# A two-layer kernel on one core: the context rows' expert products at 256 columns a strip instead of 128

## The chip, the cores and the metric

The kernel runs on one core of a Trainium2 chip. TensorE multiplies, VectorE, ScalarE and GpSimd do the rest, SyncE starts most of the transfers. The metric is the device time of one execution in microseconds (us); the kernel before takes 4492.06 us, the median of three runs.

## The reference

Two blocks are computed one after the other on 1024 rows of width 1024. The second block has two layers, each with a mixer and an expert layer of 16 experts. In its first layer 256 extra rows, the context, go through the same experts. What the change touches is this function, called for the 1024 rows (128 rows to an expert) and, in the first layer alone, for the 256 context rows (32 rows to an expert):

```
def expert_choice_ffn(h, w_router, w1, w3, w2):
    cap = EC_FACTOR * n_tok // N_EXPERTS        # 2*1024/16 = 128, context: 2*256/16 = 32
    aff = softmax(h @ w_router)
    gate, idx = top_k(swapaxes(aff, 1, 2), cap)
    xs = h[idx]
    a = xs @ w1[e];  b = xs @ w3[e]             # w1, w3: 1024 x 1024
    y = (silu(a) * b) @ w2[e] * gate            # w2: 1024 x 1024
    return zeros.at[idx].add(y)
```

All is float32.

## The kernel before

The stage is `block_moe_quads(cr, l)`. Expert 0 and expert 15 are written out, and experts 1 to 14 are one loop body (`Fori(1, NE - 1)`), on each engine.

An expert's weights come as six tiles of 2048 KB, `W[0]` to `W[5]`. Tiles 0 to 3 hold W1 and W3: tile `2c + r` has the columns of hidden half `c` (512 of 1024) for the rows of contraction half `r`, W1 in its first four slots and W3 in the last four. Tiles 4 and 5 are W2, half of its 1024 output columns each. SyncE loads the tiles of the next expert in the order 0, 3, 2, 1, 4, 5, each when its last reader is done (`free`); tiles 4 and 5 wait for `k_r`, the end of the context rows' last product.

The 128 rows of an expert are multiplied by a scheme of seven half-size products (`product_1` to `product_7`, all through `pair`, line 3362), with sums of weight tiles on VectorE (`sum_0`, `sum_1`, `sum_3`, `sum_4`, lines 3629, 3637, 3644, 3651), transposes of the result (`turn_hidden`, line 3302), and `down` (line 3392) for W2.

The 32 context rows of an expert fill only 32 of the array's 128 columns of weights. So four products run side by side, one on each strip of 32 (`s` in 0 to 3), each with its own columns of the weight tile moving and its own 32 partitions of the result:

- `ctx_up` (line 3333): W1 and W3. For each hidden half `c`, each of W1 and W3 (`h`), eight steps of the contraction (`k`) and four strips, a matmul that moves 128 columns: 128 matmuls. It waits for tiles 0 and 1 before `c = 0`, for 2 and 3 before `c = 1`.
- `ctx_hidden` on VectorE multiplies the two results, TensorE transposes them (line 3302), ScalarE copies them to `hid_c` (line 3548).
- `ctx_down` (line 3354): W2. Two halves of the output, eight steps, four strips, 128 columns each: 64 matmuls.
- `out_ctx` (line 3682) scales them, and GpSimd adds them to `x_rows` in DRAM (line 3292).

To let strip `s` hold the output columns 256 s to 256 s + 255, the host stores W2 of the first layer with its columns in another order (`pieces`), and `out`, which scales the 128 rows' result, puts them back with a strided write (`part`, `whole`, line 3670). The order on TensorE in an expert is `ctx_up`, the seven products with the transposes between them, `down` twice, `ctx_down`.

Each float32 matmul is two passes in the trace, each with a weight load of its own: the 128 matmuls of `ctx_up` are 256 MATMUL and 256 LDWEIGHTS records.

Of the kernel before, what the change touches and what calls it, by code (L numbers as in the profile page):

```python
# [22 lines left out]
ALU = mybir.AluOpType  # L23
AXX = mybir.AxisListType.X

P = 128
D = 1024
SEQ = 1024
KT = D // P
# [15 lines left out]
HB = 16  # L45
# [3100 lines left out]
def expert_tile(cr, j):  # L3146

    return cr.at((25600, 17024, 29696)[j - 3], TILE)


def block_moe_quads(cr, l):
# [3 lines left out]
    nc = cr.nc  # L3155
    ctx = l == 0
# [21 lines left out]
    yr = cr.at(8320, D)  # L3178
    mrow = cr.at(9600, D)
    diag = cr.at(1024, 2, D)  # L3180
    sa_c, hg_c, hid_c, mrow_c, x_c, yc = (cr.at(a, 256) for a in (4608, 4864, 6144, 6400, 6656, 9344))
    x_c, hid_c = (v.rearrange("p (k t) -> p k t", k=KT) for v in (x_c, hid_c))
    xcT, xgc = cr.at(10880, NE, KT, CAPC), cr.at(14976, 2, D)
    T0, T1 = cr.at(33792, KT, 512), cr.at(21120, KT, 512)
    W = [(cr.ring[:, SLOT[w0 + j], :] if j < 3 else expert_tile(cr, j)).rearrange("p (k n) -> p k n", k=KT) for j in range(6)]
    B11, B21, B12, B22 = W[0:4]
    sm = cr.small
    ix, gt = sm[:, S_IX:S_IX + NE].bitcast(U32), sm[:, S_GT:S_GT + NE]
    ixg, ixs, gtc = sm[:, S_IXG:S_IXG + 4].bitcast(U32), sm[:, S_IXC:S_IXC + NE].bitcast(U32), sm[:, S_GTC:S_GTC + NE]
    gcol, scol, mcol = (GS_2L0, GS_2L1)[l], MC_L + 48 * l + 24, MC_L + 48 * l + 40  # L3190
    AB, BB, CB, HB, YB = 0, 1, 2, (4, 5), (6, 7)
    TB = CB, 3
    UB, KB = 3, HB[0]
    TURNS = ((0, made11, (0, 0), HB), (1, made12, (0, 1), (BB, 3)), (3, made22, (1, 1), HB), (2, made21, (1, 0), (AB, BB)))

    def rows(r, u):
# [3 lines left out]
    def loaded(eng, j, e):  # L3200

        if j < 3:
            eng.wait_ge(cr.loaded[SLOT[w0 + j]], 16 * USE[w0 + j] + 16 * e)
        else:
            eng.wait_ge(cr.late_tiles[j - 3], 16 * e + 16)

    def some(e):

        return not isinstance(e, int) or e > 0

    def part(v, h):

        return v.rearrange("p (s h c) -> p h s c", s=4, h=2)[:, h] if ctx else v[:, h * 512:(h + 1) * 512]

    def whole(bank):
        return bank.rearrange("p (s c) -> p s c", s=4) if ctx else bank

    with nc.Block(no_gpsimd_drain=True) as block:
        @block.sync
# [77 lines left out]
        def _(pe):  # L3297
# [26 lines left out]
            def ctx_up(e):  # L3324

                pe.wait_ge(xc, e + 1)
                for c in range(2):
                    for r in range(2):
                        loaded(pe, 2 * c + r, e)
                    for h in range(2):  # L3330
                        for k in range(KT):
                            for s in range(4):
                                last = nc.tensor.matmul(cr.bank[UB][32 * s:32 * s + 32, (2 * h + c) * P:(2 * h + c + 1) * P], x_c[:, k],  # L3333
                                                        W[2 * c + k // 4][:, 4 * h + k % 4, s * P:(s + 1) * P],
                                                        start=(k == 0), stop=(k == KT - 1), skip_group_check=True)
                last.then_inc(u_r, 1)

            def ctx_hidden(e):
# [9 lines left out]

            def ctx_down(e):

                for h in range(2):
                    for k in range(KT):
                        for s in range(4):
                            last = nc.tensor.matmul(cr.bank[KB][32 * s:32 * s + 32, h * P:(h + 1) * P], hid_c[:, k], W[4 + h][:, k, s * P:(s + 1) * P],
                                                    start=(k == 0), stop=(k == KT - 1), skip_group_check=True)
                last.then_inc(k_r, 1)

            def pair(bank, left, right, start):
# [101 lines left out]
            def body_ctx(e, with_x, first=False):  # L3460

                pe.wait_ge(x_link, 3 * e + 1)
                ctx_up(e)
                product_1(e)
                product_2(e)
                if first:
                    ctx_turn(1)
                product_6(e)
                if first:
                    ctx_turn(2)  # L3470
                product_5(e)
                if first:
                    ctx_turn(3)
                product_3(e)
                product_7(e)
                turn_hidden(e, 0)
                turn_hidden(e, 1)
                ctx_hidden(e)
                product_4(e)
                turn_hidden(e, 2)  # L3480
                if with_x:
                    turn(e + 1)
                turn_hidden(e, 3)
                down(e, 0)
                down(e, 1)
                ctx_down(e)
# [113 lines left out]
        def _(dve):  # L3600
            tt, ts, stt = nc.vector.tensor_tensor, nc.vector.tensor_scalar, nc.vector.scalar_tensor_tensor
# [60 lines left out]
            def gate_of(table, e):  # L3662
                return table[:, e:e + 1] if isinstance(e, int) else table[:, bass.ds(e, 1)]

            def out(e, h):

                dve.wait_ge(c_r, 2 * e + (h + 1))
                if h == 0 and some(e):
                    dve.wait_ge(sc, SC * e)
                stt(part(yr, h), whole(cr.bank[YB[h]][:, :]), gate_of(gt, e), part(mrow, h), ALU.mult, ALU.mult).then_inc(c_e, 1)  # L3670

            def ctx_hidden(e):

# [33 lines left out]
            def body(e, with_x):  # L3707

                block_11(e)
                half_12(e)  # L3710
                sum_4(e)
                block_12(e)
                block_22(e)
                for g in range(4):
                    hidden(e, g)
                if with_x:
                    place(e + 1)
                    row_sums(e + 1)
                    sum_0(e + 1)
                    out(e, 0)  # L3720
                    sum_1(e + 1)
                    sum_3(e + 1)
                    out(e, 1)
                else:
                    out(e, 0)
                    out(e, 1)
# [498 lines left out]
def block_final(cr):  # L4225
# [10 lines left out]
    with nc.Block(no_gpsimd_drain=True) as block:  # L4236
# [20 lines left out]
        def _(dve):  # L4257
# [11 lines left out]

BLOCKS = [block_first, block_ssm, block_a_out, block_kv, block_bq, block_fox, block_bout,  # L4270
          block_ein, block_window, block_eout, lambda cr: block_router(cr, 0), lambda cr: block_moe_quads(cr, 0),
          block_oin, block_oup, block_mla, block_oout, lambda cr: block_router(cr, 1), lambda cr: block_moe_quads(cr, 1), block_final]


# [17 lines left out]
def _tiles(w, cols=512):  # L4292

    K, N = w.shape
    out = []
    for c in range(0, N, cols):
        part = w[:, c:c + cols]
        if part.shape[1] < cols:
            part = np.concatenate([part, np.zeros((K, cols - part.shape[1]), np.float32)], 1)
        out.append(part.reshape(K // P, P, cols).transpose(1, 0, 2).reshape(P, -1))  # L4300
    return out
# [13 lines left out]
def lay_out(i):  # L4315
    i = {k: np.asarray(v) for k, v in i.items()}
# [7 lines left out]
    e = i["ev_w_in_2"][0]  # L4324
    t += _tiles(e[:, 256:768]) + _tiles(e[:, 1280:1792]) + _tiles(e[:, 0:256]) + _tiles(e[:, 768:1280]) + _tiles(i["ev_w_out_2"][0][pair_rows()])

    pieces = np.arange(D).reshape(4, 2, P).transpose(1, 0, 2).reshape(-1)

    def moe(l):
        if l == 0:  # L4330
            t.extend(mods[28:34])
        for n in range(NE):
            w1, w3 = (_tiles(i[f"exp_{w}_2"][l, n]) for w in ("w1", "w3"))
            w2 = _tiles(i["exp_w2_2"][l, n][:, pieces] if l == 0 else i["exp_w2_2"][l, n])
            rows = lambda v, r: v.reshape(P, KT, 512)[:, 4 * r:4 * r + 4].reshape(P, -1)
            t.extend([np.concatenate([rows(w1[c], r), rows(w3[c], r)], 1) for c in range(2) for r in range(2)] + w2)
    moe(0)
    o = i["od_w_in_2"][0]
    t += _tiles(o[:, 0:288]) + _tiles(o[:, 288:672])
# [7 lines left out]
    t.append(pad(kv.transpose(1, 0, 2).reshape(P, -1)))  # L4347
    t += _tiles(i["od_w_out_2"][0])
    moe(1)
    assert len(t) == N_TILES  # L4350
    a = {"wstream": np.stack(t)}
# [65 lines left out]
```

## Time and profile before

| | |
|---|---|
| median of three runs | 4492.06 us |
| lowest, highest | 4484.34, 4494.48 us |
| the profiled execution, span | 4462.5 us |
| TensorE busy | 4110.1 us (92%) |
| VectorE busy | 2364.5 us (53%) |
| ScalarE busy | 1132.6 us (25%) |
| expert stage of the first layer | about 2120 to 2970 us |

The profile is of one execution, and its page gives the span, from the first to the last instruction, as that execution's own time; no other time of it is shown. The medians of the runs lie 29.6 us above the span. Busy time is the union of an engine's records: where four matmuls run side by side it counts once. PE is TensorE's matmuls, PEld its weight loads, DVE VectorE, ACT ScalarE, POOL GpSimd, SPq the transfers that SyncE starts. "<-" names what ended an idle time; "issue" is time for which the profile shows nothing that was waited for.

### The profile page before, as it was taken

What the parts mean: (1) busy time and instruction counts of PE and PEld (TensorE: products, weight loads), DVE (VectorE), ACT (ScalarE), POOL (GpSimd) and SP (SyncE); (2) the same over time, 40 slices, a digit from 0 to 9 for tenths busy, and PEclk for the clock granted to TensorE, in tenths of its full rate; (3) what the DMA queues carried; (4) which work ended last, traced back from release to release, by engine and by line L of the source; (5) the groups of instructions that cost most, each with busy time, mean ns of one, the idle gap of its engine ahead of it and who ended that gap; (6) DMA issues with size and microseconds to landing.
All of it is one profiled execution on the core that took longest, in us unless ns stands there. A gap on an engine that the chain in (4) does not pass through costs nothing. (4 is left out here: it accounts for less than half of the span.)

```text
span 4462.5 us, 74337 instructions
## 1 busy us (share of the span) xinstructions
PE 4110.1 (92%) x30096; PEld 2628.8 (59%) x30096; DVE 2364.5 (53%) x4884; ACT 1132.6 (25%) x2569; POOL 230.0 (5%) x281
## 2 busy tenths in 40 slices
PE   7996899999899999996999999989989995999997
PEld 4443756888667788674555445558757773333332
DVE  6408334433676554746555555534435556666664
ACT  2011222212575323832200001021135632000001
POOL 0100000000121000000000000000000000000000
PEclk9998999999999999997999999999999997999998
DMA  7658221132421112116567767740161114888986
GB/s 292 242 89 344 76 76 39 67 107 94 164 91 67 74 61 97 33 58 267 226 248 272 281 256 279 269 155 21 60 209 43 21 59 166 323 341 326 344 332 224
DMA packets 133594, 757.41 MB, mean 170 GB/s; under 512 B 14336, under 2 KB 52992, under 8 KB 97904
## 3 DMA queue, kind: packets, MB, share of 16 engines
q1 hardware_dynamic: 108048, 670.05, 40.1%
q0 software_dynamic: 20272, 64.76, 5.3%
q10 hardware_dynamic: 5040, 19.37, 1.2%
q8 instruction: 161, 2.64, 0.2%
q14 instruction: 73, 0.60, 0.0%
HBM read 663.46 MB, written 91.19 MB: 169 GB/s over the span
## 5 line engine op out<-in xcount | busy, mean ns | idle before, releaser
L440 PE MATMUL psum<-w_ring,arena 128*128 128x256 f32 (+1 forms) x2784 | 610.7, 378 | 19.8 <-PEq L199 8.5
L440 PEld LDWEIGHTS psum<-w_ring,arena 128*128 128x128 f32 x2784 | 522.8, 192 | 91.1 <-issue 21.2
L3362 PE MATMUL psum<-arena 128*64 128x512 f32 x2048 | 452.5, 593 | 2.6
L3392 PE MATMUL psum<-arena 128*128 128x512 f32 x1024 | 447.9, 595 | 3.7 <-DVE arena L3659 0.9
L440 PE MATMUL psum<-arena,w_ring 128*128 128x256 f32 x1600 | 352.9, 380 | 6.4 <-DVE arena L495 3.5
L3362 PE MATMUL psum<-w_ring,arena 128*64 128x512 f32 x1536 | 343.8, 597 | 2.8 <-issue 2.8
L3392 PEld LDWEIGHTS psum<-arena 128*128 128x128 f32 x1024 | 191.9, 190 | 237.6 <-issue 231.2
L440 PEld LDWEIGHTS psum<-arena,w_ring 128*128 128x128 f32 x1600 | 301.8, 190 | 49.5 <-DVE w_ring L536 3.6
L3362 PEld LDWEIGHTS psum<-arena 128*64 128x64 f32 x2048 | 150.8, 137 | 273.1 <-issue 271.0
L3510 ACT ACTIVATE arena<-psum 128x512 f32<-128x512 f32 x128 | 76.6, 598 | 911.6 <-PE psum L3362 911.6
L1851 PE MATMUL psum<-arena 48*128 48x512 f32 (+5 forms) x1440 | 292.1, 516 | 8.9 <-PEq L1464 3.5
L1920 ACT ACTIVATE arena<-psum 128x512 f32<-128x512 f32 (+3 forms) x436 | 195.1, 483 | 207.8 <-PE psum L1870 197.9
L1928 ACT ACTIVATE arena<-arena,small 128x640 f32<-128x640 f32 (+8 forms) x272 | 244.6, 900 | 7.4 <-DVE small L1979 7.3
L506 DVE TENSOR_TENSOR arena<-arena,psum 128x256 f32<-128x256 f32 (+1 forms) x92 | 38.5, 418 | 386.5 <-PE psum L440 386.5
L3362 PEld LDWEIGHTS psum<-w_ring,arena 128*64 128x64 f32 x1536 | 108.2, 137 | 219.4 <-issue 219.4
L412 PE MATMUL psum<-arena,w_ring 128*128 128x512 f32 (+1 forms) x560 | 231.6, 566 | 0.0
L1894 PE MATMUL psum<-arena 128*64 128x128 f32 x3104 | 207.2, 274 | 17.1 <-DVE arena L1800 10.3
L3644 DVE TENSOR_TENSOR w_ring<-arena,w_ring 128x4096 f32<-128x4096 f32 x32 | 141.5, 4420 | 106.3 <-PE psum L3333 106.3
L1894 PEld LDWEIGHTS psum<-arena 128*64 128x64 f32 x3104 | 179.7, 137 | 29.3 <-issue 20.5
L1870 PEld LDWEIGHTS psum<-consts,arena 64*128 64x128 f32 x3104 | 133.2, 139 | 105.9 <-issue 60.8
L440 PE MATMUL psum<-arena 128*128 128x256 f32 x768 | 173.5, 381 | 9.1 <-DVE arena L495 8.6
L1870 PE MATMUL psum<-consts,arena 64*128 64x64 f32 x3104 | 156.5, 228 | 22.8 <-ACT arena L1920 7.6
(429 smaller groups left out, 5376.9 us busy)
## 6 DMA issues: line engine op xcount, KB each, us to landing
w_ring<-in_wstream SPq DMA_DIRECT2D x162, 2048.0 KB, 10.3
arena<-in_wstream SPq DMA_DIRECT2D x97, 2048.0 KB, 7.8
x_rows<-arena SPq DMA_DIRECT2D x26, 512.0 KB, 2.7
w_ring<-in_wstream ACTq DMA_DIRECT2D x6, 2048.0 KB, 7.8
arena<-x_rows SPq DMA_DIRECT2D x18, 512.0 KB, 7.3
xn_rows<-arena POOLq DMA_DIRECT2D x18, 512.0 KB, 7.3
arena<-f_rows SPq DMA_DIRECT2D x8, 1024.0 KB, 7.6
arena<-x_rows SPq DMA_DIRECT2D x8, 1024.0 KB, 9.1
```

What stands on the lines that cost most here:

```text
L412: last = cr.nc.tensor.matmul(bank_ap, l, r, start=(k == 0), stop=(k == len(pairs) - 1))
L440: last = self.cr.nc.tensor.matmul(out, l, r, start=(start and k == 0), stop=(k == len(pairs) - 1), skip_group_check=True)
L506: self.cr.nc.vector.tensor_tensor(to, to, self.c(n), ALU.add).then_inc(self.made12, 1)
L1851: last = nc.tensor.matmul(cr.bank[2 * h + C % 2][:, 0:p.b - p.a], s_.q(h)[j], p.keys(h)[j], start=(j == 0), stop=(j == parts - 1))
L1870: last = nc.tensor.transpose(cr.bank[4 + r][:, at:at + HD], s_buf[rows, s % 3, h, col:col + P], cr.const(C_ID)[rows, rows])
L1894: nc.tensor.matmul(o[h * HD:(h + 1) * HD], s_.pv[blk][1](h), t_buf[:, h, g, n * P:(n + 1) * P], start=(blk == 0), stop=(blk == len(s_.pv) ...
L1920: copy = lambda to, of: nc.scalar.activation(to, of, ACT.Copy)
L1928: nc.scalar.activation(v, v, ACT.Exp, bias=shift_of(s, h), scale=-1.0, accum_out=rsum[:, s % 3, h:h + 1]).then_inc(pr, 1)
L3362: last = nc.tensor.matmul(cr.bank[bank][HT * h:HT * (h + 1), :], left[:, k], right[:, 4 * h + k, :], start=(start and k == 0), stop=(k == ...
L3392: last = nc.tensor.matmul(cr.bank[YB[h]][:, :], hid[:, k], W[4 + h][:, k, :], start=(k == 4), stop=(k == 3))
L3510: nc.scalar.activation(blk[i], cr.bank[of][:, :], ACT.Copy).then_inc(kept, 1)
L3644: tt(B12, B22, B12, ALU.subtract).then_inc(t_3, 1)
```

## The change

The context rows' matmuls move 256 columns each instead of 128. In `ctx_up` strip `s` now takes the hidden columns 256 s to 256 s + 255, which lie in hidden half `s // 2`, so that the loop over `c` is gone and all four tiles are waited for at the start. There are 64 matmuls where there were 128. In `ctx_down` there are 32 where there were 64; the index of `hid_c` changes with the order in which the hidden values now come. W2 is stored in its natural order, and `out` writes its half without strides. What the four strips read together is the same as before, the same bank and the same 512 (or 256) columns of it are written, and no buffer, semaphore or transfer is added or taken away.

```diff
-    UB, KB = 3, HB[0]
+    UB, KB, QW = 3, HB[0], 256
     def part(v, h):
-        return v.rearrange("p (s h c) -> p h s c", s=4, h=2)[:, h] if ctx else v[:, h * 512:(h + 1) * 512]
-
-    def whole(bank):
-        return bank.rearrange("p (s c) -> p s c", s=4) if ctx else bank
+        return v[:, h * 512:(h + 1) * 512]
             def ctx_up(e):
                 pe.wait_ge(xc, e + 1)
-                for c in range(2):
-                    for r in range(2):
-                        loaded(pe, 2 * c + r, e)
-                    for h in range(2):
-                        for k in range(KT):
-                            for s in range(4):
-                                last = nc.tensor.matmul(cr.bank[UB][32 * s:32 * s + 32, (2 * h + c) * P:(2 * h + c + 1) * P], x_c[:, k],
-                                                        W[2 * c + k // 4][:, 4 * h + k % 4, s * P:(s + 1) * P],
-                                                        start=(k == 0), stop=(k == KT - 1), skip_group_check=True)
+                for j in range(4):
+                    loaded(pe, j, e)
+                for h in range(2):
+                    for k in range(KT):
+                        for s in range(4):
+                            last = nc.tensor.matmul(cr.bank[UB][32 * s:32 * s + 32, QW * h:QW * (h + 1)], x_c[:, k],
+                                                    W[s // 2 * 2 + k // 4][:, 4 * h + k % 4, QW * (s % 2):QW * (s % 2 + 1)],
+                                                    start=(k == 0), stop=(k == KT - 1), skip_group_check=True)
             def ctx_down(e):
-                for h in range(2):
-                    for k in range(KT):
-                        for s in range(4):
-                            last = nc.tensor.matmul(cr.bank[KB][32 * s:32 * s + 32, h * P:(h + 1) * P], hid_c[:, k], W[4 + h][:, k, s * P:(s + 1) * P],
-                                                    start=(k == 0), stop=(k == KT - 1), skip_group_check=True)
+                for k in range(KT):
+                    for s in range(4):
+                        last = nc.tensor.matmul(cr.bank[KB][32 * s:32 * s + 32, 0:QW], hid_c[:, 4 * (k % 2) + k // 2],
+                                                W[4 + s // 2][:, k, QW * (s % 2):QW * (s % 2 + 1)],
+                                                start=(k == 0), stop=(k == KT - 1), skip_group_check=True)
-                stt(part(yr, h), whole(cr.bank[YB[h]][:, :]), gate_of(gt, e), part(mrow, h), ALU.mult, ALU.mult).then_inc(c_e, 1)
+                stt(part(yr, h), cr.bank[YB[h]][:, :], gate_of(gt, e), part(mrow, h), ALU.mult, ALU.mult).then_inc(c_e, 1)
-    pieces = np.arange(D).reshape(4, 2, P).transpose(1, 0, 2).reshape(-1)
-            w2 = _tiles(i["exp_w2_2"][l, n][:, pieces] if l == 0 else i["exp_w2_2"][l, n])
+            w2 = _tiles(i["exp_w2_2"][l, n])
```

On TensorE, from the jump into the loop to the first of the seven products, there stands before (32x128 is 32 rows by 128 columns of the result; REGISTER_ALU works out a semaphore's value for a wait):

```order
917 L3499 UNCONDITIONAL_BRANCH
918 L3499 ISA
919 L3326 REGISTER_ALU
920 L3203 ISA
921 L3203 REGISTER_ALU
922 L3333 MATMUL psum<-w_ring,arena 32x128 x64
923 L3203 REGISTER_ALU
924 L3205 REGISTER_ALU
925 L3333 MATMUL psum<-w_ring,arena 32x128 x16
926 L3333 MATMUL psum<-arena 32x128 x16
```

and after the change, with all the work for the waits now ahead of the first matmul and 18 + 2 + 2 matmuls in the place of 64, the ring's and the arena's tiles taking turns by pairs of strips:

```order
929 L3495 UNCONDITIONAL_BRANCH
930 L3495 ISA
931 L3323 REGISTER_ALU
932 L3203 ISA
933 L3203 REGISTER_ALU x2
934 L3205 REGISTER_ALU
935 L3329 MATMUL psum<-w_ring,arena 32x256 x18
936 L3329 MATMUL psum<-arena 32x256 x2
937 L3329 MATMUL psum<-w_ring,arena 32x256 x2
```

At the loop's end TensorE has before, from the second half of `down` to the first product of the written-out expert 15:

```order
948 L3392 MATMUL psum<-arena 128x512 x12
949 L3354 MATMUL psum<-arena 32x128 x64
950 L3499 REGISTER_ALU
951 L3499 COMPARE_AND_BRANCH
952 L3333 MATMUL psum<-w_ring,arena 32x128 x80
```

and after it:

```order
970 L3388 MATMUL psum<-arena 128x512 x12
971 L3349 MATMUL psum<-arena 32x256 x32
972 L3495 REGISTER_ALU
973 L3495 COMPARE_AND_BRANCH
974 L3329 MATMUL psum<-w_ring,arena 32x256 x18
```

So 96 of an expert's matmuls are gone, nothing else is moved past anything else, and the other engines' instructions stand as they did.

## Rows read from the trace of the kernel before

**Rows 1.** The page's head: the span, TensorE's and VectorE's busy time.

```profile
span 4462.5 us, 74337 instructions
PE 4110.1 (92%) x30096; PEld 2628.8 (59%) x30096; DVE 2364.5 (53%) x4884; ACT 1132.6 (25%) x2569; POOL 230.0 (5%) x281
```

**Rows 2.** Busy time by stretch; columns as in the header row.

```profile
core 0: us, PE busy (x) PEld busy (x) DVE busy (x) ACT busy (x) POOL busy (x), PEclk, DMA share, GB/s
2240.00:2905.00 665.00, 663.54 (x7433) 339.06 (x7424) 360.74 (x364) 59.58 (x143) 52.27 (x38) 1.00 0.71 269
3810.00:3860.00 50.00, 49.76 (x215) 20.01 (x214) 35.97 (x34) 3.63 (x8) 2.58 (x2) 1.00 0.90 339
```

**Rows 3.** Waits in the first layer's expert stage: total us, times, longest.

```profile
ACT arena L3540 <- PE psum L3333: 380.4, 16, 27.2
DVE w_ring L3644 <- PE psum L3333: 106.3, 16, 9.3
DVE arena L3682 <- PE psum L3354: 45.3, 16, 2.9
PE psum L3333 <- issue: 8.2, 3, 3.6
```

**Rows 4.** TensorE's timeline over one expert of the loop: start, us, instructions.

```profile
2342.45 4.57 PE L3333 MATMUL psum<-w_ring,arena 128*32 128x128 f32 x160
2346.83 1.06 PE L3333 MATMUL psum<-arena 128*32 128x128 f32 x32
...
2348.58 1.06 PE L3333 MATMUL psum<-arena 128*32 128x128 f32 x32
2349.57 7.09 PE L3362 MATMUL psum<-w_ring,arena 128*64 128x512 f32 x32
2356.49 10.47 PE L3362 MATMUL psum<-arena 128*64 128x512 f32 x48
2366.79 3.60 PE L3362 MATMUL psum<-w_ring,arena 128*64 128x512 f32 x16
...
2390.20 3.70 PE L3354 MATMUL psum<-arena 128*32 128x128 f32 x128
2393.84 4.57 PE L3333 MATMUL psum<-w_ring,arena 128*32 128x128 f32 x160
```

**Rows 5.** TensorE's timeline ahead of the stage: 128 and 256 columns, whole and strips.

```profile
1984.26 5.34 PE L440 MATMUL psum<-w_ring,arena 128*128 128x256 f32 x24
1989.44 1.04 PE L364 MATMUL psum<-consts,arena 128*128 128x128 f32 x8
1990.31 1.89 PE L440 MATMUL psum<-w_ring,arena 128*128 128x256 f32 x8
...
1996.01 1.07 PE L2245 MATMUL psum<-arena 128*32 128x256 f32 x16
1997.01 1.99 PE L440 MATMUL psum<-arena 128*128 128x256 f32 x8
```

**Rows 6.** The timeline at the loop's first expert and after its last.

```profile
2185.42 4.55 PE L3333 MATMUL psum<-w_ring,arena 128*32 128x128 f32 x160
2193.34 1.08 PE L3333 MATMUL psum<-w_ring,arena 128*32 128x128 f32 x32 [2.50 <-issue]
...
2907.84 4.55 PE L3333 MATMUL psum<-w_ring,arena 128*32 128x128 f32 x160
2916.61 0.84 PE L3333 MATMUL psum<-arena 128*32 128x128 f32 x19 [2.06 <-issue]
```

**Rows 7.** DMA queues of 2190 to 2192, 2910 to 2915, 3810 to 3860 us: packets, MB, share.

```profile
q8 instruction: 1, 0.02, 4.2%
...
q8 instruction: 1, 0.02, 1.1%
...
q8 instruction: 2, 0.03, 0.2%
```

**Rows 8.** DMA queues of 2240 to 2905 us, all of them.

```profile
q1 hardware_dynamic: 11232, 163.58, 60.2%
q0 software_dynamic: 5598, 15.26, 10.6%
q14 instruction: 1, 0.01, 0.0%
```

**Rows 9.** SyncE's transfers over the same expert as rows 4.

```profile
2370.57 0.91 SPq L3226 DMA_DIRECT2D w_ring<-in_wstream  x2
2394.10 0.87 SPq L3226 DMA_DIRECT2D arena<-in_wstream  x2
```

**Rows 10.** `out` on VectorE in the first layer, then in the second: count, ns min/median/max.

```profile
L3670 DVE SCALAR_TENSOR_TENSOR arena<-psum,small,arena x32: 741/743/750, 2177.1 to 2958.3; 128x512 f32<-128x512 f32 x32
...
L3670 DVE SCALAR_TENSOR_TENSOR arena<-psum,small,arena x32: 740/742/751, 3816.1 to 4430.5; 128x512 f32<-128x512 f32 x32
```

## The prediction

> **What bounds the kernel now.** I read the page's head first, then busy time by stretch, then the waits of the stage, and last TensorE's timeline over one expert. The head gives a span of 4462.5 us with TensorE busy 92% and VectorE 53% [rows 1]. In the loop of the first layer's experts TensorE is busier still: 663.54 of 665 us, at the full clock of 2.4 GHz, with VectorE at 360.74 us and the DMA engines at 0.71 [rows 2]. The waits say the same from the other side: ScalarE waits 380.4 us and VectorE 106.3 us for `ctx_up`, and VectorE 45.3 us for `ctx_down`, while TensorE waits 8.2 us in all before a matmul of `ctx_up`, three times, for nothing that the profile names [rows 3]. So what TensorE saves here moves the end one for one, and what the others save is worth nothing.
>
> One expert of the loop takes 2393.84 - 2342.45 = 51.39 us [rows 4]. Of it `ctx_up` has 2349.57 - 2342.45 = 7.12 us and `ctx_down` 2393.84 - 2390.20 = 3.64 us. These 10.76 us, 172 us over 16 experts, are all that the change works on.
>
> **Term 1: fewer, longer matmuls.** Four strips run together, so the unit is a group of four passes. In `ctx_up` 160 passes, or 40 groups, take 2346.83 - 2342.45 = 4.38 us from start to start: 109.5 ns a group of 128 columns [rows 4]. What a group of 256 columns takes I read from passes of that width. On the whole array, 24 passes of 256 columns take 1989.44 - 1984.26 = 5.18 us: 215.8 ns each; eight of 128 columns take 1990.31 - 1989.44 = 0.87 us: 109 ns [rows 5]. Two strips at 512 columns take 2366.79 - 2356.49 = 10.30 us for 24 pairs, 429.2 ns a pair [rows 4]. So width alone sets the time: 109, 216 and 429 ns, whether whole, in two strips or in four. From 128 to 256 columns a pass grows by 106.3 ns, and of the 109.5 ns about 3 are a fixed cost of the group. One group of 256 in place of two of 128 saves 219.0 - 215.8 = 3.2 ns. There are 32 such groups in `ctx_up` and 16 in `ctx_down`, 48 an expert, 768 in all: 2.5 us.
>
> Bounds. The trace has four strips at 256 columns once: 16 passes, 1.07 us, with 1.00 us from their start to the next line's start [rows 5]. A run of eight groups of 128 columns goes from its start to the products' start in 2349.57 - 2348.58 = 0.99 us [rows 4], of which 8 x 109.5 = 876 ns are the groups and 114 ns the change over to the wider shape. If the change over costs as much here, 886 ns remain for four groups: 221.5 ns, and the term is (219.0 - 221.5) x 768 = 1.9 us lost. With nothing taken off at all, 1.07 us / 4 = 267 ns, 37 us lost. At the other end a group without any fixed cost is 2 x 106.3 = 212.6 ns, and the term is 4.9 us gained. I take 215.8 ns: the one run of four strips is short and bears the entry from the full array, which `ctx_up` and `ctx_down` pay once each, before as after, while 24 passes average it out.
>
> A rule on this stands in the Trainium skill, page "TensorEngine Tiling (Array Packing)", section "Instruction Overhead": each matmul has about 60 cycles of overhead. By it, as an estimate, 192 passes fewer an expert would save 60 / 2.4 = 25 ns each, 77 us in all. The trace speaks against that: a pass takes 109.5 / 4 = 27.4 ns altogether, and the array's own share, 106.3 / 4, leaves under 1 ns.
>
> **Term 2: two stalls of TensorE.** Of the 8.2 us, 2.50 us stand at 2190.84 us, in `ctx_up` of the loop's first expert, and 2.06 us at 2914.55 us, in `ctx_up` of the written-out expert behind the loop [rows 6]. Both are in the middle of a run of matmuls without a wait on data. At both a packet of the instruction queue lands inside or just ahead of the gap, while the weight tiles keep the DMA engines busy [rows 7]; from 2240 to 2905 us, while the loop repeats, TensorE's instruction queue (q8) has not one packet, and there is no such stall [rows 8, 2]. So these are the two places where code is new to the core, and `ctx_up` runs through it fastest: 27.4 ns a pass, against 215 ns in the products. The third part of the 8.2 us, 3.6 us [rows 3], is the wait of expert 0 for its copied rows, and stays.
>
> In the first stall TensorE had gone through 192 passes in 5.4 us and got the next code 2193.34 - 2185.42 = 7.9 us after its start. After the change the same amount of code is 128 passes of 54 ns and 64 of 215 ns, 6.9 + 13.8 = 20.7 us. In the second it is 237 passes (160 + 32 + 32 + 13; two rows between repeat those of rows 4) and the code came 8.8 us after the start; after the change they last 6.9 + 109 x 0.215 = 30 us. The products cover a fetch: in the second layer's loop, without context rows, two packets of instructions fall into 3810 to 3860 us with the DMA share at 0.90, and TensorE is busy 49.76 of 50 us [rows 7, 2]. So I take both stalls as gone: 4.56 us. Bounds: none gone, 0; a new boundary of code that falls badly could cost a stall of the same size, 2.5 us.
>
> The Trainium skill, page "Runtime: NRT & Kernel Launch", section "Instruction fetch mechanics", says that each engine refills its instruction memory in blocks of 16 KiB, and that a taken branch whose target is not there stalls until the block has come. The trace agrees on both loop ends and on the block (rows 7: 0.02 MB a packet). Taken as it stands the rule speaks against this term, since the branches remain; by it the sum would be term 1 alone. That is rival B.
>
> **What costs nothing.** The waits for tiles 2 and 3 move ahead by half of `ctx_up`, 3.5 us. The last two of tiles 0 to 3 are issued at 2370.57 us [rows 9], and the last of the four is tile 1, for which `ctx_up` waited at its start already; the start is at 2393.84 us, 23.3 us after the issue. On SyncE tiles 4 and 5 are issued right behind `ctx_down` (2394.10), so they start with it, 0.05 us earlier, and have until the next `down`. `out` without strides: 743 ns with them in the first layer and 742 ns without in the second [rows 10]. The end of `ctx_up` releases ScalarE and VectorE, which both wait for it by microseconds. Moving the waits' register work ahead of the matmuls adds nothing that shows: TensorE's sequencer runs ahead of the array, and the 3.64 us of `ctx_down` hold the same kind of work and a branch in 3640 - 32 x 109.5 = 136 ns.
>
> **The sum.** 2.5 + 4.56 = 7.1 us off the span: 4462.5 - 7.1 = 4455.4 us. The median of the runs lies 29.6 us above the span, so 4492.06 - 7.1 = 4485 us.
>
> **The rivals.**
> A, the forecast: both terms, 4485 us.
> B, the stalls stay, whole or in part, or come up elsewhere, since some thousand instructions fewer shift where each block of code begins. For: the branches remain. Against: the slower passes and the second layer's loop. Time: 4492.06 - 2.5 = 4489.6 us.
> C, slower: four strips of 256 columns, each its own stream out of two tiles at once, take longer than two groups of 128. Place: all 768 groups. Price: 0.77 us for each ns above 219. It decides from 231 ns on, where 9 us are lost; at the 267 ns of the bound it is 4492 + 37 = 4529 us, less the stalls. For: the one run of this shape gives 221.5 ns, not 215.8. Against: even that is far from 231.
> D, a larger gain: no fixed cost in the longer groups, and the stalls gone: 4.9 + 4.56 = 9.5 us, 4482.6 us. The page on tiling would put the gain higher still; the trace leaves no room for more.
> E, the change does nothing that shows, 4492 us: it would need 219 ns a group and both stalls.
>
> **How the numbers follow.** A 0.62, B 0.20, D 0.07, C 0.07, E 0.04. About 0.2%, 9 us, is what a measurement of this kernel can tell from no change; the three runs before lie 10 us apart. A's 7.1 us is 0.16%, just inside: of its 0.62 I give 0.24 to faster, 0.38 to same. D gives 0.06 to faster. B gives 0.02 to faster and 0.17 to same. C gives 0.05 to slower and the rest to same. E is same. That is faster 0.32, same 0.62, slower 0.06. A's and D's runs spread by 5 us to either side of 4482 to 4485, B reaches to 4494: the range is 4477 to 4494 us.
>
> **What would show it.** Right: `ctx_up` has 128 records of MATMUL an expert and takes 32 x 0.2158 + 0.13 = 7.0 us from its start to the first product (7.12 before), `ctx_down` 3.6 us (3.64 before), an expert of the loop 51.2 us (51.39 before); the "issue" gaps at the first `ctx_up` of the loop and behind the loop are under 0.3 us. Wrong: groups start further apart than 219 ns; the two gaps are there again, or one stands in the products; TensorE waits for a transfer at the start of `ctx_up`; a stage behind 2970 us has another length than before by more than 2 us.

## The result, and the profile after

The changed kernel takes 4464.91 us (median of five runs) against 4492.06 us: a ratio of 0.9941, 95% interval 0.9929 to 0.9953. It gained 27 us, where 7.1 us were forecast, and the time lies below the range. A second comparison, six runs of the changed kernel against 23 of the kernel before, gives 0.9931 (0.9917 to 0.9944), 31 us.

First the expert stage, which goes as it was predicted. The profile after, its head:

```profile
span 4465.3 us, 68193 instructions
```

Then TensorE's timeline around one expert of the loop, with GpSimd's and SyncE's rows between (start us, us, engine, line, instructions; 3349 is `ctx_down`, 3329 `ctx_up`, 3358 the products, 3285 and 3289 the writes of rows to `x_rows`, 3266 the gather of the next rows):

```profile
2342.51 3.66 PE L3349 MATMUL psum<-arena 128*32 128x256 f32 x64
2343.86 1.57 POOL L3285 DMA_INDIRECT x_rows<-arena,small  x1 [44.99 <-DVE arena L3666]
2345.99 2.11 PE L3329 MATMUL psum<-w_ring,arena 128*32 128x256 f32 x34
2346.38 0.86 SPq L3223 DMA_DIRECT2D arena<-in_wstream  x2
2347.12 1.57 POOL L3289 DMA_INDIRECT x_rows<-arena,small  x1 [1.68 <-DVE arena L3678]
...
2348.99 1.01 POOL L3266 DMA_INDIRECT arena<-xn_rows,small  x1 [0.30 <-issue]
...
2353.01 7.09 PE L3358 MATMUL psum<-w_ring,arena 128*64 128x512 f32 x32
...
2393.63 3.66 PE L3349 MATMUL psum<-arena 128*32 128x256 f32 x64
2397.11 2.11 PE L3329 MATMUL psum<-w_ring,arena 128*32 128x256 f32 x34
```

`ctx_up` takes 2353.01 - 2345.99 = 7.02 us (7.12 before, [rows 4]; 7.0 forecast), `ctx_down` 2345.99 - 2342.51 = 3.48 us (3.64; 3.6 forecast), and an expert 2397.11 - 2345.99 = 51.12 us (51.39; 51.2 forecast). The waits of the stage (total us, times, longest) answer to [rows 3]:

```profile
ACT arena L3536 <- PE psum L3329: 370.2, 16, 24.3
DVE w_ring L3640 <- PE psum L3329: 96.2, 16, 6.5
PE psum L3329 <- DVE arena L3615: 3.6, 1, 3.6
```

The two gaps of 2.5 and 2.1 us are gone. Only the 3.6 us before the first `ctx_up` are left, as forecast. TensorE's busy time of 2240 to 2905 us, with the columns of [rows 2], is as full as it was:

```profile
2240.00:2905.00 665.00, 663.61 (x5049) 287.56 (x5052) 361.83 (x365) 59.56 (x143) 53.84 (x39) 1.00 0.71 269
```

So every step of the forecast can be seen, and yet the span is 4465.3 us, no less than the 4462.5 us of [rows 1]. The first and the last matmul records of the stage, before and then after, say where the difference lies (ns min/median/max, first to last start in us):

```profile
L3333 PE MATMUL psum<-w_ring,arena x3072: 269/273/423, 2128.0 to 2913.9; 128*32 128x128 f32 x192
L3354 PE MATMUL psum<-arena x2048: 272/273/298, 2181.9 to 2961.6; 128*32 128x128 f32 x187
...
L3329 PE MATMUL psum<-w_ring,arena x1536: 376/379/634, 2136.3 to 2915.0; 128*32 128x256 f32 x192
L3349 PE MATMUL psum<-arena x1024: 379/379/404, 2189.1 to 2959.4; 128*32 128x256 f32 x171
```

Within the stage the changed kernel is 10.5 us shorter. Ahead of the stage its profile is 8.3 us longer and behind it 5.0 us, where no instruction was changed. Over all 14 profiles, of whatever kernel, the part ahead of the stage takes 2128.0 to 2140.0 us and the part behind it 1500.2 to 1508.2 us, and two profiles of the same kernel differ by 2.0 to 2.5 us in each (2128.0 and 2130.0 us ahead of it in the kernel before). So one span against one other can't show a gain of a few microseconds. The 5.0 us are over the 2 us that the prediction named as a sign of being wrong. What makes these parts longer or shorter, no run here shows; but the times gained by 27 and 31 us, and the stage alone, as the later profiles have it, by 28.8, so little is left for them.

The run that this profile belongs to took 4467.19 us: 1.9 us lie around the span, not 29.6. If the same holds for the profile of before, with a span of 4462.5 us, it came from an execution of about 4464 us, while every timed run of that kernel took 4480 us or more. The profile that I read was not of the kind of execution that is timed. What did the others have in them?

### The profile page after: what moved, and what is told of

It is laid out like the page before. It is cut to its first block and busy times, and to the rows that moved or that the text cites. A ratio compares the mean times of both kernels' runs of the same rounds, so it can differ in the third digit from the quotient of the medians.

```text
span 4465.3 us, 68193 instructions
## 1 busy us (share of the span) xinstructions
PE 4116.9 (92%) x27024; PEld 2569.5 (58%) x27024; DVE 2364.5 (53%) x4884; ACT 1132.7 (25%) x2569; POOL 229.9 (5%) x281
```

## The experiments

I call the stage the time from the first matmul record of `ctx_up` to the start of the last record of `ctx_down`. It is 2961.6 - 2128.0 = 833.6 us in the profile of before and 2959.4 - 2136.3 = 823.1 us after. Expectations that speak of 830, 849 and 820 us counted up to the start of the last `ctx_down`, some 3.5 us less. The two stalls at the loop's entry and behind its exit are not the same length in every profile (`ctx_up` of expert 1 takes 8.66 to 11.73 us in the kernels with 128 columns in it), so a stage is good to 2 us or so. The length of an expert inside the loop is steadier: in the median 51.42 us in the profile of before and 51.12 after.

**Both kernels again.** No edit.

> The unchanged kernel, timed against itself, to get a second profile of it. Theory 1 (the stage explains about 10 us, and the rest of the 27 us is not in the expert stage): ratio 1.000 within 0.001, and a profile whose expert stage, from the first matmul of ctx_up of expert 0 to the last ctx_down, takes 830 us as in the profile on record, with the stalls of 2.5 and 2.1 us; if its time is near 4490 us, the 25 us over the profile on record stand elsewhere. Theory 2 (the profile on record was a lucky execution of the stage): the stage is 10 to 25 us longer than 830 us, with stalls in more experts than two or longer ones.

> The changed kernel again, on this chip. Theory 1: ratio 0.994 again, stage of 820 us. Rival (the 27 us were mostly chance, of a chip or of where buffers lie): the ratio is near 0.9977, 10 us.

The kernel before against itself: 0.9999 (0.9991 to 1.0008), 4493.61 us. The changed one: 0.9931, stage 824.1 us. So the gain is there again, and the interval rules out the 0.9977 of chance. The new profile of before has a span of 4486.1 us and is the key to the case. Its first and last matmul records of `ctx_up` and `ctx_down` (ns min/median/max, first to last start, us):

```profile
L3333 PE MATMUL psum<-w_ring,arena x3072: 269/273/421, 2130.0 to 2932.6; 128*32 128x128 f32 x192
...
L3354 PE MATMUL psum<-arena x2048: 269/273/298, 2183.0 to 2982.9; 128*32 128x128 f32 x187
```

A stage of 852.9 us, 19 us longer than in the execution of [rows 1]: theory 2. Its timeline over one expert of the loop, with the weight loads (PEld), which show a pause better than matmuls that overlap:

```profile
2395.05 2.33 PEld L3354 LDWEIGHTS psum<-arena 128*32 128x32 f32 x85 [0.76 <-issue]
2396.40 1.58 POOL L3288 DMA_INDIRECT x_rows<-arena,small  x1 [46.10 <-DVE arena L3670]
2397.70 1.24 PEld L3354 LDWEIGHTS psum<-arena 128*32 128x32 f32 x43 [0.32 <-issue]
2399.06 1.90 PEld L3333 LDWEIGHTS psum<-w_ring,arena 128*32 128x32 f32 x71
...
2400.12 1.55 POOL L3292 DMA_INDIRECT x_rows<-arena,small  x1 [2.15 <-DVE arena L3682]
2401.44 1.46 PEld L3333 LDWEIGHTS psum<-w_ring,arena 128*32 128x32 f32 x52 [0.48 <-issue]
...
2401.98 1.01 POOL L3269 DMA_INDIRECT arena<-xn_rows,small  x1 [0.30 <-issue]
2403.25 1.04 PEld L3333 LDWEIGHTS psum<-w_ring,arena 128*32 128x32 f32 x37 [0.35 <-issue]
...
2407.10 7.09 PE L3362 MATMUL psum<-w_ring,arena 128*64 128x512 f32 x32
```

`ctx_up` takes 2407.10 - 2399.06 = 8.04 us and `ctx_down` 4.01 us. The passes between are no slower than in [rows 4] (43 weight loads in 1.24 us); the time is in three pauses of 0.32, 0.48 and 0.35 us with no releaser, 1.15 us of the 1.3 us that the expert is longer. And each of the three comes behind the start of an indirect transfer on GpSimd (one whose rows are given by a list of indices): work resumes 1.30, 1.32 and 1.27 us after it. Over the stage there are 45 such pauses, one for each indirect transfer that starts while the context rows' matmuls run, and all of them end 1.25 to 1.33 us after its start. An expert of the loop takes 52.72 us in the median, where it took 51.42. From here on I had theory P (an indirect transfer holds up TensorE's supply of instructions, and matmuls of 128 columns have no reserve for it) against theory Q (a pause of TensorE's own stream, at a fixed place in it).

**Only `ctx_up` at 256 columns.** `ctx_down` and W2 stay as they were, but for `hid_c`'s index.

```diff
-  hid_c[:, k], W[4 + h][:, k, s * P:(s + 1) * P]
+  hid_c[:, 4 * (k % 2) + k // 2], W[4 + h][:, k, s * P:(s + 1) * P]
```

> Only ctx_up moves 256 columns; ctx_down keeps 128 columns and W2 its old order. Theory 1 (time saved where the trace shows it): both stalls gone (4.6 us) and 16 x 0.1 us of groups, 6 to 7 us of the stage, ratio about 0.9985 if nothing else moves. Theory 2 (more stalls of instruction fetch in ctx_up than the profile on record shows): most of the 27 us, ratio 0.995.

4476.06 us, ratio 0.9965 (0.9953 to 0.9978), stage 834.9 us, 18 us less. `ctx_up` has no pauses, and of the stalls 0.07 and 0.14 us are left at the loop's entry and exit; the pause in `ctx_down` is still there. Theory 1's 0.9985 is missed; theory 2's 0.995 is nearer and just outside the interval.

**Only `ctx_down` at 256 columns**, with W2 in natural order; `ctx_up` as before.

```diff
-  hid_c[:, 4 * (k % 2) + k // 2],      # of the changed kernel
+  hid_c[:, k],
```

> Only ctx_down moves 256 columns, W2 in natural order, out without strides; ctx_up as before. Theory 1: 16 x 0.16 us = 2.6 us of the stage, both stalls of ctx_up still there, ratio 0.9994. Rival (natural order of W2 or the plain write of out is worth something that the profile did not show): 10 us or more, ratio under 0.998.

0.9984 (0.9975 to 0.9993), stage 844.7 us, 8 us less: between the two expectations. The two pauses in `ctx_up` and its stalls stay. Alone the two edits gain 18 and 8 us of the stage, both at once 28.8 (852.9 - 824.1). Most of the missing 2.6 us can be seen: with only `ctx_up` changed, `ctx_down` takes 4.22 us in the loop instead of 4.03, by a longer gap between its last pass and the next expert's first. In that place all the work for the waits now stands, ahead of the first matmul, and the prediction had said that it adds nothing that shows. Whether it is this work, no run tells apart; with both edits the gap is gone.

**Only the natural order** of W2 and the plain write of `out`; all matmuls at 128 columns:

```diff
-  W[4 + h][:, k, s * P:(s + 1) * P]
+  W[4 + s // 2][:, k, QW * (s % 2) + h * P:QW * (s % 2) + (h + 1) * P]
```

> Only W2's natural order and the plain write of out; ctx_up and ctx_down keep 128 columns a matmul. Theory P: no part of the gain comes from it; pauses as in the kernel before, stage 849 us, ratio 1.000 within 0.001. A rival (order of W2 or write of out worth something): ratio 0.998 or less.

1.0001 (0.9992 to 1.0009), stage 850.0 us, an expert of the loop 52.76 us. It is worth nothing, as said.

**The kernel before without indirect writes in the first layer.** The rows go to fixed places, so this kernel and the next two compute another result; they are here for the time alone.

```diff
-  pool.indirect_dma_start(out=x_d[:, :], out_offset=..ix[:, e:e + 1].., in_=yr, compute_op=ALU.add)
+  pool.dma_start(x_d[0:P, :], yr)
-  pool.indirect_dma_start(out=x_q[:, :], out_offset=..ixs[:, e:e + 1].., in_=yc, compute_op=ALU.add)
+  pool.dma_start(x_q[4 * P:5 * P, :], yc)
```

> The kernel before, but in the first layer both writes of an expert's rows to x_rows are plain transfers of the same size from GpSimd's queue to fixed rows, so the result is another one; the gather of the next expert's rows stays an indirect transfer. In a second profile of the kernel before, ctx_up takes 8.05 us instead of 7.12 and ctx_down 4.04 instead of 3.65 in every expert, by pauses of about 0.3 to 0.4 us in TensorE's row of matmuls, each beginning 0.84 to 0.98 us after GpSimd starts an indirect transfer. Theory P (an indirect transfer on GpSimd holds up TensorE's supply of instructions for some 0.9 us, and matmuls of 128 columns have no reserve for it): the pause in ctx_down and the first one of ctx_up are gone, the second of ctx_up, behind the gather, stays; the stage is about 12 us shorter, ratio 0.9975. Theory Q (the pauses are of TensorE's own instruction stream, by its position, and the match in time is chance): nothing changes, ratio 1.000.

0.9973 (0.9964 to 0.9982), stage 838.9 us, 14.0 us less. The timeline of the same place:

```profile
2343.67 3.43 PEld L3354 LDWEIGHTS psum<-arena 128*32 128x32 f32 x128 [0.76 <-issue]
...
2345.04 0.55 POOL L3288 DMA_DIRECT2D x_rows<-arena  x1 [46.73 <-DVE arena L3670]
2347.31 2.77 PEld L3333 LDWEIGHTS psum<-w_ring,arena 128*32 128x32 f32 x102 [0.20 <-issue]
...
2348.34 0.55 POOL L3293 DMA_DIRECT2D x_rows<-arena  x1 [2.75 <-DVE arena L3682]
2349.19 1.00 POOL L3269 DMA_INDIRECT arena<-xn_rows,small  x1 [0.30 <-issue]
2350.46 1.56 PEld L3333 LDWEIGHTS psum<-w_ring,arena 128*32 128x32 f32 x57 [0.38 <-issue]
```

The 128 weight loads of `ctx_down` run in one piece. `ctx_up` has one pause, and it has moved with the gather: at its 102nd weight load, no longer at the 123rd, ending 1.27 us after the gather's start. The gather adds nothing to what it writes, so the addition of the two writes isn't needed for a pause. Theory Q has the place fixed, and falls.

**And without the indirect gathers** of experts 1 to 15:

```diff
+  if ctx and e: pool.dma_start(xg, xn_d[0:P, :]).then_inc(gx, 16)
```

> The same with the gathers of experts 1 to 15 as plain loads of fixed rows too, so that the first layer's loop has no indirect transfer. Theory P: all three pauses gone, ctx_up 7.12 us and ctx_down 3.65 us in every expert of the loop, stage 18 to 20 us shorter than in the second profile of before, ratio 0.9957. Theory Q: 1.000.

0.9956 (0.9941 to 0.9971), stage 833.9 us, 19.0 us less. The loop looks as in [rows 4] again:

```profile
2396.19 4.57 PE L3336 MATMUL psum<-w_ring,arena 128*32 128x128 f32 x160
2397.22 0.55 POOL L3296 DMA_DIRECT2D x_rows<-arena  x1 [2.77 <-DVE arena L3685]
2397.76 0.54 POOL L3274 DMA_DIRECT2D arena<-xn_rows  x1
2400.58 1.06 PE L3336 MATMUL psum<-arena 128*32 128x128 f32 x32
...
2402.32 1.06 PE L3336 MATMUL psum<-arena 128*32 128x128 f32 x32
2403.32 3.23 PE L3365 MATMUL psum<-w_ring,arena 128*64 128x512 f32 x14
```

7.13 us for `ctx_up`, and 51.43 us for an expert of the loop in the median. What is left in this kernel are the two stalls of new code, under "issue" in its waits:

```profile
PE psum L3336 <- issue: 4.3, 2, 2.5
```

**The same edit to the changed kernel**, the control:

> The same edit to the changed kernel, as a control of what the plain transfers themselves are worth. Theory P: the changed kernel has no pauses to lose, so its stage stays at 820 us and the ratio to before stays at 0.9931, within 0.001. If the ratio falls by another 0.004, the plain transfers gain time for a reason of their own, and the two runs before say nothing on pauses.

0.9935 (0.992 to 0.995), stage 824.0 us, against 0.9931 and 824.1 with indirect transfers. At 256 columns they cost TensorE nothing, and the plain transfers gain nothing by themselves. All three pauses are the doing of GpSimd's indirect transfers, and the width hides them. This kernel's waits name only the 3.6 us before expert 0:

```profile
PE psum L3332 <- issue: 3.6, 1, 3.6
```

**The width as a dose.** The changed kernel, `ctx_down` alone in other widths:

```diff
+  for h in range(n):     # (w, n, step): (64, 4, 64), (96, 3, 80), (160, 2, 96)
+      matmul(cr.bank[KB][.., w * h:w * (h + 1)], .., W[4 + s // 2][:, k, QW * (s % 2) + step * h:QW * (s % 2) + step * h + w], ..)
```

> The changed kernel with ctx_down in 64 columns a matmul: four quarters, 128 matmuls, 256 passes instead of 64; same result. Theory P: TensorE has a reserve of some 20 passes, which last 0.28 us at 64 columns, so the pause behind the row scatter is 0.6 us or more in ctx_down (0.33 at 128 columns, 0 at 256), unless a floor of issue above 14 ns a pass already sets the pace; then the passes start further apart than 14 ns and ctx_down is well over 4 us. By a fixed cost of 3 ns a group alone ctx_down would be 64 x 56.3 ns + 0.13 = 3.7 us.

> The changed kernel, but ctx_down moves 96 columns a matmul in three steps that overlap (columns 0, 80 and 160 on), so some are computed twice and their place in the result is not the reference's. At 64 columns the pauses in ctx_down add up to 1.0 us, at 128 to 0.33. With a stop T of the supply and a reserve of R passes of 13.9, 20.6, 27.4, 34 ns, a pause is T - R x pass: the two widths give R = 52 and T = 1.75 us. Then 96 columns pause 0.68 us. With the reserve of 20 passes and the stop of 0.9 us that I put down before, it is 0.49 us.

> The same with 160 columns in two steps (columns 0 and 96 on). With R = 52 and T = 1.75 us the reserve lasts 52 x 34 = 1.77 us and there is no pause; with 20 passes and 0.9 us it is 0.22 us.

At 64 columns the timeline reads:

```profile
2347.74 1.61 PEld L3350 LDWEIGHTS psum<-arena 128*32 128x32 f32 x112 [0.76 <-issue]
...
2349.10 1.57 POOL L3285 DMA_INDIRECT x_rows<-arena,small  x1 [45.71 <-DVE arena L3667]
2349.66 0.17 PEld L3350 LDWEIGHTS psum<-arena 128*32 128x32 f32 x6 [0.30 <-issue]
...
2350.41 2.04 PEld L3350 LDWEIGHTS psum<-arena 128*32 128x32 f32 x138 [0.58 <-issue]
```

112 weight loads in 1.61 us are 14 ns a pass: the pace still follows the width at half of what it was before. The pause, in two pieces, adds up to 1.0 us beyond the steady pace, and work resumes in full 1.31 us after the transfer's start. The jump back costs more here too: `ctx_down` takes 5.33 us in the median of the loop and 4.92 us in expert 14, behind which TensorE doesn't jump. At 96 columns (83 ns a group):

```profile
2397.61 2.29 PE L3350 MATMUL psum<-arena 128*32 128x96 f32 x93
2398.96 1.58 POOL L3285 DMA_INDIRECT x_rows<-arena,small  x1 [45.61 <-DVE arena L3667]
2400.28 2.34 PE L3350 MATMUL psum<-arena 128*32 128x96 f32 x99 [0.38 <-issue]
2400.28 2.12 PEld L3350 LDWEIGHTS psum<-arena 128*32 128x32 f32 x98 [0.58 <-issue]
```

The pause is 0.70 us by the starts of the groups (0.68 by the fit, 0.49 by my first guess), and it ends 1.32 us after the start. At 160 columns all 128 matmul passes come without a pause (their weight loads still stop for under 0.1 us, at the same 1.3 us after the start, and no matmul is late for it):

```profile
2394.93 4.76 PE L3350 MATMUL psum<-arena 128*32 128x160 f32 x128
2396.27 1.58 POOL L3285 DMA_INDIRECT x_rows<-arena,small  x1 [45.01 <-DVE arena L3667]
```

So 1.0, 0.70, 0.33 and 0 us at 64, 96, 128 and 160 columns: the end stands still at 1.3 us after the transfer's start, and the pause shrinks as the passes grow. That looks like a stream of instructions that is held up for a time, and a reserve of passes that lasts longer as they grow. The straight line through the first two points (52 passes, 1.75 us) forecast the other two, and my guess of 20 passes did not. But its two numbers can't be taken for the mechanism's. A stop of 1.75 us that ends 1.31 us after the transfer's start would begin 0.44 us ahead of it, and VectorE's instruction that GpSimd waited for ended only 0.29 us ahead. And the weight loads stop for the same 0.58 us at 64 and at 96 columns; only the piece before it shrinks, from 0.30 to 0.11 us. How large the reserve is stays open.

In time 64 columns lost all of the gain: 1.0005 (0.9995 to 1.0016), stage 853.8 us. The versions with 96 and 160 columns were timed once each (4490.32 and 4483.98 us). Their steps overlap, so they move 288 and 320 columns where 256 are needed and compute another result; their times say nothing on the pauses.

**512 columns.** `ctx_up` with W1's and W3's columns in one matmul:

```diff
+  of = W[s // 2 * 2 + k // 4].rearrange("p (h k) n -> p k h n", h=2)[:, k % 4, :, QW * (s % 2):QW * (s % 2 + 1)]
+  matmul(cr.bank[UB][32 * s:32 * s + 32, :].rearrange("p (h n) -> p h n", h=2), x_c[:, k], of, ..)
```

> The changed kernel with ctx_up in 512 columns a matmul: one matmul moves the 256 columns of W1 and the 256 of W3 behind each other, so 32 matmuls in the place of 64; same result. Theory P: no pause is left to save, only the fixed cost of a group: 32 groups of 216 ns become 16 of 429, 2.7 ns each, 0.04 us an expert, 0.7 us in all: ratio 0.993, as the changed kernel. If code fetch or pauses still cost something at 256 columns, more.

0.9929 (0.9916 to 0.9942), stage 822.6 us. An expert takes 2395.38 - 2344.29 = 51.09 us against 51.12:

```profile
2344.29 4.03 PE L3329 MATMUL psum<-w_ring,arena 128*32 128x512 f32 x34
...
2395.38 4.03 PE L3329 MATMUL psum<-w_ring,arena 128*32 128x512 f32 x34
```

The trace shows the small gain; the runs can't tell this version from the changed kernel.

## Why the prediction was wrong

The direction was right, and what it said of the stage holds. By its steps:

- **What bounds the kernel**: right. TensorE is the bound of the stage, and what it saved arrived: 28.8 us of stage, 27 and 31 us of time.
- **Term 1, a group's cost**: 215.8 ns was right for `ctx_up` (7.12 to 7.02 us, 0.10 forecast). `ctx_down` gained 0.16 us instead of 0.05. It took 3.52 us in experts 0 and 14, behind which TensorE doesn't jump back, and 3.64 to 3.68 in the others of the loop; so 0.12 us or more of the jump stood open behind passes of 27 ns and is hidden behind those of 54. The 3.48 us after are the same with a jump and without. I had seen the 136 ns and taken them for a cost that stays. The bound of 221.5 ns was the entry from the full array, as argued: after the change the groups start 216 ns apart.
- **Term 2, two stalls of new code**: right in place and size. They are in `no_indirect` (4.3 us) and not in `a_no_indirect`. That they wait for code is read from the packets of [rows 7]; no run changed the code's place alone. By the rule of the Trainium skill that the prediction cites (page "Runtime: NRT & Kernel Launch", section "Instruction fetch mechanics": a taken branch whose target is not there stalls) they would have stayed, since the branches do. The prediction said that the trace agrees; that went too far. Both stalls stand behind the loop's ends, 192 and 237 passes on, with no such stall at the jump itself, and the loop's exit is not a taken branch. The runs show that the pace of what is executed can hide them.
- **What costs nothing**: right (`natural`: 1.0001).
- **The sum**: this step failed. "The median of the runs lies 29.6 us above the span, so 4492.06 - 7.1": I took the difference as time around the span that no change touches. Only 1.9 us are that. The rest was a sign that the profiled execution lacked something the timed ones have, and most of that was in the very matmuls that the change works on: three pauses an expert, 19.0 us in all (852.9 - 833.9 us of stage; 52.72 - 51.43 = 1.29 us an expert of the loop), absent in [rows 4] and so in every term. The other 8 to 9 us of the 29.6 lie outside the stage and in the spread of the runs. No rival named the pauses, since each was built on durations of that one execution.

Put together, with stages of the later profiles: 852.9 (before) to 833.9 us (without indirect transfers) is 19.0 us of pauses; 833.9 to 824.0 us (without them, and at 256 columns) is 9.9 us, where 7.1 were forecast: the two stalls, and 51.43 - 51.12 = 0.31 us an expert where term 1 had 0.16. Their sum, 28.9 us, is between the two measured gains of 27 and 31 us.

That the indirect transfers make the pauses is shown: the pauses go with them, move with the gather, and the control gains nothing. That the width hides them is shown by the changed kernel and the four widths. That what is held up is TensorE's supply of instructions is argued from this pattern; no view shows the supply. By which path a GpSimd transfer reaches TensorE, no run here shows. And why the execution on record ran without pauses, with the same three transfers at the same places, is open, so the transfers are needed for the pauses but not enough for them: 77 timed runs of the kernel before, the fastest 4482.22 us, and its second profile do not show that kind again.

## What to carry to other kernels

Before working out a change from a profile, hold the profile's span against the timed runs: if the gap is more than the few us that lie around a span (1.9 us here, where 29.6 were read), the profile may be of another kind of execution, and another profile of the same kernel is worth more than any estimate. Where many short matmuls run side by side, think of the instructions in flight as a reserve in time: here a stream of 27 ns passes paused at each indirect transfer of GpSimd, at new code, and at the jump of a loop, and one of 54 ns passes at none of them. Fewer, wider matmuls can gain ten times what their fixed cost says: 27 us here, where the fixed cost alone said 2.5.

## What the runs showed of the hardware

- An indirect transfer that GpSimd starts (1.58 us on its engine for the writes, 1.0 us for the gather) can stop TensorE's weight loads and matmuls for 0.3 to 1.0 us, until 1.3 us after its start. It did so at 14, 21 and 27 ns a pass; at 34 and 54 ns no matmul was late. A plain transfer from the same queue (0.55 us) did not. In one profile of the kernel before, at 27 ns a pass, the indirect transfers did not either.
- Four strips side by side keep up with 14 ns a pass, weight load and matmul each, at 64 columns (56 ns a group).
- At the full granted clock a group of float32 passes side by side takes its columns (106 ns for 128) and 3 to 4 ns: with four strips at 64, 96, 128, 160, 256 and 512 columns (56, 83, 109.5, 136, 216 and 429 ns), and likewise with two strips at 512 and the whole array at 128 and 256.
